# A hybrid decoder layer on one core: fewer products in the mLSTM heads, an unsplit value product and a mask filled by GpSimd in the prompt attention, and moved steps in the later stages

## The chip, the core and the metric

One core of a Trainium2 chip runs the whole program. The time is the device time of one execution, in microseconds; the shown figure is the median of three runs. Its engines are TensorE (PE in the profile, with PEld for its weight loads), VectorE (DVE), ScalarE (ACT), GpSimd (POOL) and SyncE (SP, which here only issues DMAs). Each has its own queue of instructions and works it off in order; semaphores make one wait for another.

## The reference

One layer for 1024 prompt positions of one sequence and for 8 decoding sequences of 4 new positions each (32 columns, kept behind the 1024). What matters here:

```python
def mlstm_chunk(carry, xs):           # 4 heads of 128, chunks of 128 positions
    ...
    s = jnp.einsum('bhtd,bhsd->bhts', q, k) * w_intra
    num = w_inter[..., None] * jnp.einsum('bhtd,bhde->bhte', q, c_st) + jnp.einsum('bhts,bhse->bhte', s, v)
    den = w_inter * jnp.einsum('bhtd,bhd->bht', q, n_st) + jnp.sum(s, axis=-1)
    h = num / jnp.maximum(jnp.abs(den), jnp.exp(-m_t))[..., None]
    ...
    n_new = decay[..., None] * n_st + jnp.einsum('bhs,bhsd->bhd', w_s, k)

def fox_prompt(q, k, v, lf):          # 8 heads of 64, blocks of 128 rows
    ...
    logits = logits + fb.transpose(0, 2, 1)[..., None] - f_keys[:, :, None, :]
    logits = jnp.where(kpos[None, :] <= qpos[:, None], logits, -jnp.inf)
    p = jax.nn.softmax(logits, axis=-1)
    return jnp.einsum('bhts,bshd->bthd', p.astype(v.dtype), v)

def merge_out(x, y_m, m_o, g_mh, y_f, gates, w_pa, w_pb, w_out):
    hm = rmsnorm(y_m.astype(x.dtype), g_mh) * jax.nn.sigmoid(m_o).reshape(bn, t, H_M, DV_M)
    a = hm.reshape(bn, t, W_M) @ w_pa
    b = y_f.reshape(bn, t, W_F) @ w_pb
    return x + (jax.nn.sigmoid(ga) * a + jax.nn.sigmoid(gb) * b) @ w_out

def ffn_and_ple(x, p, g_ffn, w_gu, w_down, g_ple, w_ple_gate, w_ple_proj):
    ...
    gate = jax.nn.sigmoid(rmsnorm(x, g_ple) @ w_ple_gate)
    return x + gate * (p.astype(x.dtype) @ w_ple_proj)
```

`fox_sample` is the same attention for the new positions, with keys, values and forget values of 512 earlier positions read from pages of a cache.

## The kernel before

All of it is float32. Most products are made of three: each operand is split into a high half in the reduced format fp32r and the low rest (names that end in h and l, as `wha` and `wla`), and high x high, low x high and high x low are summed. ACT or GpSimd makes a high half by a copy, VectorE or GpSimd the low half by a subtraction. The 1056 columns go in three pieces of 352; 24 products of 352 columns for one output block are called a unit here. The stages run one after the other, each engine with its own part of each, and the order on every engine is written out by hand.

**Stage 2, mLSTM and gate units (213 to 521 us).** Four heads, one after the other. For a head, VectorE weights queries (`qs`), keys (`kws`, `kw`) and scores (`sw`) and runs the chunk states (`states`, `nstates`). TensorE makes numerators in `pA` (L1917, L1919) and, with a matrix of ones, denominators in `pB` (L1920 for the scores, L1922 for the state), then the same for the 32 new positions in `pS` (L1924 to L1930, by sequence). ACT and VectorE turn the denominators into factors (`dd`, L1532, with its reciprocal) while TensorE works on gate units (L1863), and after `h_done` TensorE makes the new states (L1939, L1941).

**Stage 3, prompt attention (521 to 810 us).** Eight heads (g) of eight blocks of 128 rows (i). `logits3` makes the logits of a block against all keys up to it from split halves (L1966, L1967), and a bf16 product of `identb` and `maskb` adds the mask to the block on the diagonal (L1969). `bias3` on VectorE adds the forget row `nF` and takes the maximum in one instruction (L1559), and from it makes the exponent's bias `nb` (L1563). ACT applies the exponential (L1223), TensorE transposes (`turn_p3`, L1978), ACT copies the high half `pth` (`high3`, L1227), VectorE subtracts the low half `ptl` (`low3`, L1568), and for every second block `values3` multiplies with `vh` and `vl` (L1995). Halves of gate units (`FILL`) lie between the blocks in TensorE's queue. GpSimd makes low halves of queries (`low_q`, L902), keys (`low_k`, L908), values (`low_v`, L912) and of weight chunks (`split_chunk`, L842).

**Stage 4, decode attention (810 to 917 us).** 18 gate units are numbered f; `logits4`, `turn_p4`, `values4` for two groups of four sequences stand among them at fixed numbers. `load_pages` on SP brings in the cache pages (`kvg`).

**Stage 5, merge (917 to 1138 us).** Products with w_pb, then w_pa, then w_out (L2105). VectorE squares the mLSTM rows, normalizes them and makes the low halves `actl`; in the second loop it makes `tmp` and its low half `tl` (`low_t`, L1678) per piece t.

**Stage 6** is the FFN, which the change leaves alone. **Stage 7** (1895 to 2031 us) is the gate of the layer embedding: for each unit (c, t), block c of 8 and piece t of 3, TensorE makes gate and projection. For c = 0 it first sums the squares of the piece (`sums7`, L2199), which ACT (`sqa`) and GpSimd (`sqp`, by pairs, three buffers) prepare. ACT makes the scale (`rms7`), then the sigmoid, and VectorE the result `yq` (L1784), which frees the bank for the second unit after.

Of the kernel before, what the change touches and what calls it, by code (L numbers as in the profile page):

```python
# [22 lines left out]
P = 128  # L23
# [25 lines left out]
def program(nc, a, o):  # L49

    ctx = ExitStack()
    with ctx:
# [37 lines left out]
        identb = take("identb", [P, P], BF16)  # L90
        maskb = take("maskb", [P, P], BF16)
# [77 lines left out]
        sw = take("sw", [P, T])  # L169
        kw = take("kw", [P, NCH, DM])  # L170
# [6 lines left out]
        sqn = take("sqn", [P, 2, T])  # L177
        attn2_end = top[0]
# [5 lines left out]
        top[0] = attn3_base  # L184
        nF = take("nF", [P, 2, SEQ])
# [4 lines left out]
        pth = take("pth", [P, 20 * 256], F32R)  # L190
        ptl = take("ptl", [P, 20 * 256], F32R)
        vh = take("vh", [P, NCH, P], F32R)
        vl = take("vl", [P, NCH, P], F32R)
# [3 lines left out]
        mx = take("mx", [P, NCH])  # L197
        fcol = take("fcol", [P, NCH])
# [211 lines left out]
        v_hi = sem("v_hi")  # L410
        v_lo = sem("v_lo")
# [3 lines left out]
        nb_done = sem("nb_done")  # L415
        p_done = sem("p_done")
        tp_mm = sem("tp_mm")
        pt_hi = sem("pt_hi")
        pt_lo = sem("pt_lo")
# [70 lines left out]
        sum5 = again("sum5")  # L490
        rv_done = again("rv_done")
# [53 lines left out]
        assert IN3 % 6 == 0 and UNITS4 == 18  # L545

# [13 lines left out]
        def _(sp):  # L560
# [119 lines left out]
            def load_v(g):  # L680
                if g:
                    sp.wait_ge(v_lo, g)
                sp.dma_start(v3[:], plane(2)[0:SEQ, g * DH:(g + 1) * DH].rearrange("(i p) d -> p i d", p=P)).then_inc(v3_in, 16)
# [10 lines left out]
            def load_pages(g, first, last):  # L694

                for b in range(first, last):
                    for i in range(PAGES):
                        at_p = (g * GB + b) * PAGES + i
                        page = sp.value_load(ptb[0:1, at_p:at_p + 1], min_val=0, max_val=NPOOL - 1)
                        sp.dma_start(kvg[:, b, i, :], a["cache_kv"][bass.ds(page, 1)].rearrange("a p n -> p (a n)")).then_inc(kvg_in[g], 16)  # L700
# [19 lines left out]
            for g in range(HF):  # L720
# [3 lines left out]
                for i in range(NCH):  # L724
                    if i == 2:
                        if g:
                            store_y(g - 1)
                        if g + 1 < HF:
                            load_v(g + 1)
                    for n in chunks_ended(g, i):  # L730
                        load_chunk3(n + 3)
            for n in range(*FILL_END):
                load_chunk3(n + 3)
            sp.wait_ge(pt_in, 16)
            sp.wait_ge(nb_done, NCH * HF)
            load_pages(0, 0, GB // 2)
            store_y(HF - 1)
            sp.wait_ge(y_st, 16 * HF)
# [9 lines left out]
            load_pages(0, GB // 2, GB)  # L748
# [4 lines left out]
            sp.dma_start(gv[:], a["gains"]).then_inc(gv_in, 16)  # L753
            sp.dma_start(yst5[:, :, 0:SEQ], o["yT"].rearrange("(c p) t -> p c t", p=P)[:, :, 0:SEQ]).then_inc(y5_in, 16)
            sp.wait_ge(o4_mm, 1)
            load_pages(1, 0, GB)
# [71 lines left out]
        def _(pool):  # L828
# [20 lines left out]
            nc.gpsimd.memset(identb[:], 0.0).then_inc(pool_own, 1)  # L849
            nc.gpsimd.memset(maskb[:], 0.0).then_inc(pool_own, 1)  # L850
            nc.gpsimd.memset(maskT[:], 0.0).then_inc(pool_own, 1)
            nc.gpsimd.memset(maskS[:], 0.0).then_inc(pool_own, 1)
            pool.wait_ge(pool_own, 5)
            for m in (ident, identb):
                nc.gpsimd.affine_select(out=m[:], in_=m[:], compare_op=ALU.not_equal, fill=1.0, base=0,
                                        pattern=[[-1, P]], channel_multiplier=1)
            nc.gpsimd.affine_select(out=maskb[:], in_=maskb[:], compare_op=ALU.is_ge, fill=NEG, base=0,
# [6 lines left out]
            pool.wait_ge(pool_own, 6)  # L864
# [14 lines left out]
            for g in range(HM):  # L879
# [3 lines left out]
                pool.wait_ge(pool_own, 6 + g + 1)  # L883
# [11 lines left out]
            nc.gpsimd.memset(vh[:, :, DH:].bitcast(F32), 1.0)  # L895
            nc.gpsimd.memset(vl[:, :, DH:].bitcast(F32), 0.0).then_inc(consts, 1)

            def low_q(g, own, value):

                pool.wait_ge(qk_hi, 2 * g + 1)  # L900
                pool.wait_ge(own, value)
# [1355 lines left out]
```

## Time and profile before

| | us |
|---|---|
| median of 3 runs (lowest to highest) | 2028.18 (2027.02 to 2030.33) |
| profiled execution, device time | 2032.48 |
| span of its trace | 2030.8 |
| TensorE busy | 1935.5 (95% of the span) |
| VectorE, GpSimd, ACT busy | 864.7, 577.0, 519.5 |

The profile shows one execution. Busy time is not bound to be on the path that sets the end: TensorE's queue is nearly full, so the other engines count where TensorE waits for them. In rows with idle time, the bracket holds how long the engine stood before the instruction and who released it. The granted clock is a share of TensorE's full speed.

### The profile page before, as it was taken

The numbers are of one execution on the slowest core, as the hardware profiler recorded it, in microseconds if no ns is written. First come the engines' busy times: TensorE is split into PE (matmuls) and PEld (weight loads), VectorE is DVE, ScalarE is ACT, GpSimd is POOL, SyncE is SP. The second block draws the span as 40 slices with busy tenths as digits, with TensorE's granted clock in tenths as the row PEclk, the third lists the DMA queues.
The fourth block names the chain that finished last, engine by engine and source line by source line (L and its number), as shares of the span: only waits on it lengthen the run. The fifth ranks groups of instructions, "written<-read, shape, count | busy, mean of one in ns | idle before, by whom it ended". The sixth has DMA issues, their size and how long they took to land.

```text
span 2030.8 us, 29755 instructions
## 1 busy us (share of the span) xinstructions
PE 1935.5 (95%) x11759; PEld 1834.2 (90%) x11759; DVE 864.7 (43%) x1426; ACT 519.5 (26%) x848; POOL 577.0 (28%) x374
## 2 busy tenths in 40 slices
PE   5999999999889899988889999999999999999999
PEld 3687999999888888768889999999999999999899
DVE  3350033534467675205753344244434443443643
ACT  4421133332445453116322201000100110011710
POOL 2221112211323232112245622233222332232421
PEclk8999999889999999989999999999999999999999
DMA  5122514433434433664421211111111111111021
GB/s 175 37 74 77 171 43 160 150 103 85 134 82 105 106 95 126 215 251 172 153 87 41 83 52 42 41 41 56 47 41 41 45 58 42 41 63 37 23 91 40
DMA packets 174535, 179.14 MB, mean 88 GB/s; under 512 B 22170, under 2 KB 146142, under 8 KB 174450
## 3 DMA queue, kind: packets, MB, share of 16 engines
q1 hardware_dynamic: 156652, 155.93, 25.3%
q10 hardware_dynamic: 16774, 21.90, 3.0%
q8 instruction: 58, 0.95, 0.2%
q0 software_dynamic: 1024, 0.13, 0.1%
q14 instruction: 27, 0.22, 0.0%
HBM read 143.06 MB, written 34.87 MB: 88 GB/s over the span
## 4 chain that ended last, share of the span: by engine, by line
PE 82%; DVE 7%; issue 4%; ACT 3%; DMA 2%; SPq 1%; ACTq 1%; POOL 0%; DVEq 0%; POOLq 0%
PE pair L2105 29%; PE bank L2105 21%; PE bank L1863 13%; PE bank L1814 5%; PE pair L1995 2%; PE pair L1814 2%; DVE yb L1577 2%; DVE ptl L1568 1%; DMA kvg<-in_cache_kv 1%; PE pair L1793 1%; PE pair L1978 1%; PE pair L1875 1%; DVE actl L1422 1%; PE pair L2045 1%; PE pair L1832 1%
## 5 line engine op out<-in xcount | busy, mean ns | idle before, releaser
L1863 PE MATMUL bank<-acth,fwh 128*128 128x352 f32 x768 | 266.7, 347 | 2.9 <-DVE nrow L1545 1.9
L1863 PE MATMUL bank<-acth,fwl 128*128 128x352 f32 x768 | 255.0, 332 | 0.0
L1863 PE MATMUL bank<-actl,fwh 128*128 128x352 f32 x768 | 254.7, 332 | 0.0
L2105 PE MATMUL bank<-acth,wha 128*128 128x352 f32 x640 | 210.9, 330 | 16.5 <-DVE actl L1639 5.3
L2105 PE MATMUL bank<-acth,wla 128*128 128x352 f32 x640 | 208.4, 326 | 0.0
L2105 PE MATMUL bank<-actl,wha 128*128 128x352 f32 x640 | 208.2, 325 | 0.0
L842 POOL TENSOR_TENSOR fwl<-fraw,fwh 128x1024 fp32r<-128x1024 f32 x32 | 77.3, 2417 | 388.9 <-ACT fwh L1088 388.9
L2105 PE MATMUL pair<-hh,whb 128*128 128x352 f32 x528 | 170.7, 323 | 0.0
L2105 PE MATMUL pair<-hl,whb 128*128 128x352 f32 x528 | 169.2, 320 | 0.0
L2105 PE MATMUL pair<-hh,wlb 128*128 128x352 f32 x528 | 169.0, 320 | 0.0
L1863 PEld LDWEIGHTS bank<-acth,fwh 128*128 128x128 f32 x768 | 151.4, 197 | 9.8 <-issue 5.4
L965 POOL CAST wha<-raw 128x1024 fp32r<-128x1024 f32 x46 | 52.5, 1140 | 377.2 <-PE bank L2105 167.1
L1756 DVE TENSOR_TENSOR XR<-XR,pair 128x352 f32<-128x352 f32 x264 | 131.8, 516 | 63.1 <-PE pair L2105 63.0
L1863 PEld LDWEIGHTS bank<-actl,fwh 128*128 128x128 f32 x768 | 151.7, 198 | 1.7
L1863 PEld LDWEIGHTS bank<-acth,fwl 128*128 128x128 f32 x768 | 150.7, 196 | 0.0
L2105 PEld LDWEIGHTS bank<-acth,wha 128*128 128x128 f32 x640 | 122.5, 191 | 18.7 <-issue 16.2
L1374 ACT CAST hh<-un 128x352 fp32r<-128x352 f32 x66 | 32.2, 488 | 419.0 <-DVE un L1733 388.2
L965 POOL CAST whb<-raw 128x1024 fp32r<-128x1024 f32 x44 | 48.7, 1107 | 308.0 <-PE pair L2105 307.5
L2105 PEld LDWEIGHTS bank<-actl,wha 128*128 128x128 f32 x640 | 122.9, 192 | 0.3
L2105 PEld LDWEIGHTS bank<-acth,wla 128*128 128x128 f32 x640 | 122.5, 191 | 0.0
L967 POOL TENSOR_TENSOR wla<-raw,wha 128x1024 fp32r<-128x1024 f32 x46 | 114.2, 2483 | 3.7
L2105 PE MATMUL pair<-acth,whb 128*128 128x352 f32 x352 | 113.5, 322 | 0.0
(352 smaller groups left out, 4563.4 us busy)
## 6 DMA issues: line engine op xcount, KB each, us to landing
raw<-in_w_gu SPq DMA_DIRECT2D x44, 512.0 KB, 3.9
fraw<-in_w_in SPq DMA_DIRECT2D x32, 512.0 KB, 5.0
kvg<-in_cache_kv SPq DMA_DIRECT2D x32, 512.0 KB, 7.6
scratch_zT<-fout ACTq DMA_DIRECT2D x24, 528.0 KB, 3.5
raw<-in_w_down SPq DMA_DIRECT2D x22, 512.0 KB, 3.7
gs<-scratch_zT SPq DMA_DIRECT2D x16, 528.0 KB, 3.7
wraw<-in_w_in SPq DMA_DIRECT2D x12, 512.0 KB, 5.2
xr<-in_xT SPq DMA_DIRECT2D x6, 704.0 KB, 12.7
```

The source lines that it names most:

```text
L842: nc.gpsimd.tensor_tensor(fwl[j][:], fraw[j][:], fwh[j][:].bitcast(F32), ALU.subtract).then_inc(f_lo, 1)
L965: nc.gpsimd.tensor_copy(hi, raw[j][:]).then_inc(pool_own, 1)
L967: nc.gpsimd.tensor_tensor(lo, raw[j][:], hi.bitcast(F32), ALU.subtract).then_inc(w_split, 1)
L1374: nc.scalar.copy(hh[:, j, t * TW:(t + 1) * TW], un[:, v % 2, :]).then_inc(h_hi, 1)
L1422: nc.vector.tensor_tensor(actl[:, k, cut(t)], xn[:, k % 2, :], acth[:, k, cut(t)].bitcast(F32), ALU.subtract).then_inc(xlo_done, 1)
L1568: nc.vector.tensor_tensor(pt_view(ptl, i), tp_bank(i), pt_view(pth, i).bitcast(F32), ALU.subtract).then_inc(pt_lo, 1)
L1577: own.step(nc.vector.reciprocal(y, pC[DH:, m * 256:(m + 1) * 256]))
L1756: nc.vector.tensor_tensor(x, x, BANK[4 + u % 4][:, 0:TW], ALU.add).then_inc(x6_done, 1)
L1814: ins = nc.tensor.matmul(BANK[u % 3][0:rows, :], x[:, k, i * P:i * P + rows], w[:, q % 2, k, :], start=n == 0, stop=n == 3 * KC - 1)
L1863: ins = nc.tensor.matmul(BANK[u % 2][:, 0:TW], w[j][:, k, :], x[:, k, cut(t)], start=m == 0, stop=m == 3 * KC - 1)
L1995: ins = nc.tensor.matmul(pC[:, m * 256 + skip:(m + 1) * 256], v[:, j, :], x[:, base + j * 256 + skip:base + (j + 1) * 256], start=n == 0, ...
L2105: ins = nc.tensor.matmul(out, w[i](k), x[j](k), start=n == 0, stop=n == total - 1)
```

## The change

The causal mask of the prompt attention is filled into a copy of the forget row by GpSimd and not added by TensorE, and steps of five stages change. Part by part:

- mLSTM: VectorE makes `dn`, the scores plus queries times chunk state, and TensorE sums over it with ones in three products, 128, 384 and 512 columns. `nqs` does the same for the new positions in one product, and the new normalizer is one product with the weights in `rB`.
- Prompt attention: `masked_row` fills the mask into `nFd`, a copy of `nF`. `bias3` handles the block on the diagonal with `nFd`, the others with `nF`, and takes the larger maximum. The mask product is gone. Weights `pt` and values `vf` are no longer split: `values3` is one full float32 product per key tile; `low3` and `low_v` are gone.
- Decode attention: pages are loaded in pieces, the first four in the last but one head. `logits4(0)` stands at unit 4 in place of 6, and what follows it moves likewise. The scan of the forget values and the wait for stores `y_st` change their place.
- Merge: GpSimd squares the mLSTM rows and makes `tl` for t = 2; the sums stand after block 1 in place of 2, ACT's and VectorE's steps follow.
- Last stage: `ORDER7` puts unit (1, 0) ahead of (0, 1).

The core of the diff:

```diff
+        ORDER7 = [(0, 0), (1, 0), (0, 1), (0, 2), (1, 1), (1, 2)] + [(c, t) for c in range(2, KC) for t in range(NT)]
...
+            def masked_row(g):
+                pool.wait_ge(nF_in[g % 2], 16 * (g // 2) + 16)
+                if g >= 2:
+                    pool.wait_ge(nb_done, 8 * (g - 1))
+                nc.gpsimd.affine_select(out=nFd[:, g % 2].rearrange("p (c t) -> p c t", t=P), in_=nF[:, g % 2].rearrange("p (c t) -> p c t", t=P),
+                                        compare_op=ALU.is_ge, fill=NEG, base=0, pattern=[[0, NCH], [-1, P]],
+                                        channel_multiplier=1).then_inc(nFd_done, 1)
...
+                    if i == 2 and g + 1 < HF:
+                        masked_row(g + 1)
...
+                own.step(nc.vector.tensor_tensor(dn[:, P:].rearrange("p (c t) -> p c t", t=P), qs[:, P:SEQ].rearrange("p (c t) -> p c t", t=P),
+                                                 nstates[:, 0:NCH - 1].unsqueeze(2).to_broadcast([P, NCH - 1, P]), ALU.mult))
+                dve.wait_ge(sw_done, g + 1)
+                nc.vector.tensor_tensor(dn[:, P:], dn[:, P:], sw[:, P:SEQ], ALU.add)
...
-                own.step(nc.vector.tensor_tensor_reduce(out=lg[:, i % 2, 0:(i + 1) * P], in0=lg_bank(i), in1=nF[:, g % 2, 0:(i + 1) * P],
-                                               scale=1.0, scalar=-3.0e38, op0=ALU.add, op1=ALU.max,
-                                               accum_out=mx[:, i:i + 1]))
+                n = i * P
+                ins = nc.vector.tensor_tensor_reduce(out=lg[:, i % 2, n:n + P], in0=lg_bank(i)[:, n:n + P], in1=nFd[:, g % 2, n:n + P],
+                                                     scale=1.0, scalar=-3.0e38, op0=ALU.add, op1=ALU.max,
+                                                     accum_out=(mxd if i else mx)[:, i:i + 1])
+                if i:
+                    own.step(nc.vector.tensor_tensor_reduce(out=lg[:, i % 2, 0:n], in0=lg_bank(i)[:, 0:n], in1=nF[:, g % 2, 0:n],
+                                                            scale=1.0, scalar=-3.0e38, op0=ALU.add, op1=ALU.max,
+                                                            accum_out=mx[:, i:i + 1]))
+                    own.step(nc.vector.tensor_tensor(mx[:, i:i + 1], mx[:, i:i + 1], mxd[:, i:i + 1], ALU.max))
...
-            def square_mlstm(h):
-                dve.wait_ge(h5_in, 16)
-                nc.vector.tensor_tensor(rvm[:, h, :], hst5[:, h, :], hst5[:, h, :], ALU.mult).then_inc(hsq, 1)
...
+                if t == 2:
+                    return
...
-                for b in range(DB):
-                    ins = nc.tensor.matmul(pB[:, b:b + 1], kws[:, b, :], ones[0:NS, 0:1], start=True, stop=True)
-                ins.then_inc(us_mm, 1)
+                nc.tensor.matmul(pB[:, 0:DB], k_in[0:NS, NCH, :], rB[0:NS, SEQ + DS - 1::DS], start=True, stop=True).then_inc(us_mm, 1)
...
-                    if last:
-                        ins = nc.tensor.matmul(out[:, n - P:n], identb[:], maskb[:], start=False, stop=True)
...
-                    for v, x in ((vh, pth), (vh, ptl), (vl, pth)):
-                        ins = nc.tensor.matmul(pC[:, m * 256 + skip:(m + 1) * 256], v[:, j, :],
-                                               x[:, base + j * 256 + skip:base + (j + 1) * 256], start=n == 0, stop=n == total - 1)
-                        n += 1
+                    ins = nc.tensor.matmul(pC[:, m * 256 + skip:(m + 1) * 256], vf[:, j, :],
+                                           pt[:, base + j * 256 + skip:base + (j + 1) * 256], start=j == 0, stop=j == 2 * m + 1)
...
-                if f == 6:
+                if f == 4:
```

On TensorE, the end of the denominators of one mLSTM head, before (x8 counts instructions in a row):

```order
L1917 MATMUL pair<-sw,v_in 128x128
L1919 MATMUL pair<-qs,states 128x128
L1920 MATMUL pair<-sw,ones 128x128
L1922 MATMUL pair<-qs,nstates 128x128
L1924 MATMUL pair<-sw,v_in 128x32
L1926 MATMUL pair<-qs,cst 128x4 x8
L1928 MATMUL pair<-sw,ones 128x32
L1930 MATMUL pair<-qs,ncur 128x4 x8
```

and now the same place:

```order
L1948 MATMUL pair<-sw,v_in 128x128
L1950 MATMUL pair<-qs,states 128x128
L1951 MATMUL pair<-sw,ones 128x128
L1952 MATMUL pair<-dn,ones 128x384
L1953 MATMUL pair<-dn,ones 128x512
L1955 MATMUL pair<-sw,v_in 128x32
L1957 MATMUL pair<-qs,cst 128x4 x8
L1959 MATMUL pair<-sw,ones 128x32
L1960 MATMUL pair<-nqs,ones 128x32
```

The products with `ones` and `nstates` that alternated with the numerators are gone, and three wide ones on `dn` stand behind them.

On VectorE, block i = 3 of one head of the prompt attention, before (ISA is the reduction and its read-out):

```order
L1558 MEMSET waits 128x1
L1559 ISA lg,mx<-pair,nF 128x512
L1559 ISA mx 128x1
L1563 SCALAR_TENSOR_TENSOR nb<-mx,fcol 128x1
L1568 TENSOR_TENSOR ptl<-pair,pth 128x3x128
```

and now the same block, with `mxd` for the diagonal:

```order
L1588 MEMSET waits 128x1
L1590 ISA lg,mxd<-pair,nFd 128x128
L1590 ISA mxd 128x1
L1594 ISA lg,mx<-pair,nF 128x384
L1594 ISA mx 128x1
L1597 TENSOR_TENSOR mx<-mx,mxd 128x1
L1601 SCALAR_TENSOR_TENSOR nb<-mx,fcol 128x1
```

The subtraction for `ptl` has left the block; a second reduction with its read-out and the maximum of the two have come in ahead of `nb`.

On ACT, from the last squares of the last stage, before (rv is a scale, gn the sigmoid of a unit, yq its store):

```order
L1384 ACTIVATE acth<-XR,gv 128x352
L1387 ACTIVATE sqa<-XR 128x352
L1391 ACT_TABLE_LOAD
L1391 ACTIVATE rv_196<-pair,epsc 128x352
L1393 ACT_TABLE_LOAD
L1393 ACTIVATE rv_196<-rv_196 128x352
L1400 ACT_TABLE_LOAD
L1400 ACTIVATE gn_187<-gn_187 128x352
L1402 DMA out_outT<-yq 128x352
L1391 ACT_TABLE_LOAD
L1391 ACTIVATE rv_197<-pair,epsc 128x352
L1393 ACT_TABLE_LOAD
```

and now:

```order
L1406 ACTIVATE acth<-XR,gv 128x352
L1409 ACTIVATE sqa<-XR 128x352
L1413 ACT_TABLE_LOAD
L1413 ACTIVATE rv_196<-pair,epsc 128x352
L1415 ACT_TABLE_LOAD
L1415 ACTIVATE rv_196<-rv_196 128x352
L1421 ACT_TABLE_LOAD
L1421 ACTIVATE gn_187<-gn_187 128x352
L1423 DMA out_outT<-yq 128x352
L1421 ACTIVATE gn_191<-gn_191 128x352
L1423 DMA out_outT<-yq 128x352
L1413 ACT_TABLE_LOAD
```

The second scale now stands behind the sigmoid and the store of a second unit of the first piece.

## Rows read from the trace of the kernel before

**Rows 1.** The page's engines: busy us (share of the span) x instructions.

```profile
PE 1935.5 (95%) x11759; PEld 1834.2 (90%) x11759; DVE 864.7 (43%) x1426; ACT 519.5 (26%) x848; POOL 577.0 (28%) x374
```

**Rows 2.** TensorE's waits: line, waited for, us in total, times, longest us.

```profile
PE pair L1995 <- DVE ptl L1568: 14.6, 7, 2.3
PE pair L1966 <- DVE nb L1563: 12.1, 19, 1.8
...
PE pair L2045 <- DMA kvg<-in_cache_kv: 8.3, 2, 7.1
PE bank L2105 <- DVE tl L1678: 7.0, 1, 7.0
...
PE bank L2105 <- DVE actl L1654: 5.1, 1, 5.1
```

**Rows 3.** Timeline of TensorE, one mLSTM head: start us, us, instruction.

```profile
283.29 0.38 PE L1917 MATMUL pair<-sw,v_in 128*128 128x128 f32 x2
...
290.08 0.40 PE L1924 MATMUL pair<-sw,v_in 32*128 32x32 f32 x2
...
292.62 2.54 PE L1930 MATMUL pair<-qs,ncur 128*128 128x4 f32 x16
...
308.53 1.84 PE L1941 MATMUL pair<-ones,kws 32*128 32x1 f32 x16
```

**Rows 4.** Timeline of VectorE, the same head.

```profile
296.34 1.26 DVE L1532 TENSOR_TENSOR dd<-dd,nmB 128x1056 f32<-128x1056 f32 x1 [17.43 <-ACT dd L1192]
297.63 6.75 DVE L1533 RECIPROCAL dd<-dd 128x1056 f32<-128x1056 f32 x1
```

**Rows 5.** Windows: stretch, length, busy us of each engine, granted clock, DMA share, GB/s.

```profile
293.90:300.75 6.85, 6.85 (x27) 6.85 (x27) 4.37 (x2) 1.11 (x2) 0.00 (x0) 0.51 0.00 0
310.90:314.35 3.45, 3.45 (x13) 3.45 (x13) 1.91 (x5) 0.00 (x0) 0.35 (x1) 0.51 0.70 202
```

**Rows 6.** Timeline of TensorE in a head of the prompt attention.

```profile
592.33 0.23 PE L1969 MATMUL pair<-maskb,identb 128*128 128x128 bf16 x1
592.39 1.04 PE L1978 MATMUL pair<-ident,lg 128*128 128x128 f32 x8
...
595.79 0.39 PE L1995 MATMUL pair<-pth,vh 128*128 128x256 f32 x1 [2.05 <-DVE ptl L1568]
...
598.70 0.30 PE L1978 MATMUL pair<-ident,lg 128*128 128x128 f32 x1
```

**Rows 7.** VectorE's groups, 521 to 810 us: count, busy, mean ns, idle before.

```profile
L1563 DVE SCALAR_TENSOR_TENSOR nb<-mx,fcol 128x1 f32<-128x1 f32 x64 | 28.6, 447 | 2.3
...
L1568 DVE TENSOR_TENSOR ptl<-pair,pth 128x1024 fp32r<-128x1024 f32 x8 | 9.8, 1223 | 13.9 <-ACT pth L1227 13.9
```

**Rows 8.** Timelines of VectorE and GpSimd at 645 us.

```profile
645.58 2.21 DVE L1563 SCALAR_TENSOR_TENSOR nb<-mx,fcol 128x1 f32<-128x1 f32 x1
...
645.38 2.39 POOL L902 TENSOR_TENSOR qst<-qd,qst 64x1024 fp32r<-64x1024 f32 x1 [3.68 <-ACT qst L1234]
```

**Rows 9.** GpSimd's groups over the span, a fill of a mask.

```profile
L859 POOL TENSOR_SCALAR_AFFINE_SELECT maskT<-maskT 128x128 f32<-128x128 f32 x1 | 0.3, 288 | 0.0
```

**Rows 10.** TensorE's groups, 827 to 900 us, decode attention.

```profile
L2045 PE MATMUL pair<-kvg,qz 128*32 128x512 f32 x64 | 12.7, 968 | 8.3 <-DMA kvg<-in_cache_kv 8.3
L2063 PE MATMUL pair<-kvg,pT 128*32 128x512 f32 x32 | 3.6, 595 | 0.0
```

**Rows 11.** Timeline of VectorE in the merge.

```profile
1003.20 0.52 DVE L1678 TENSOR_TENSOR tl<-tmp,th 128x352 f32 x1
```

**Rows 12.** Timelines of TensorE, GpSimd and ACT in the last stage.

```profile
1930.27 0.43 PE L2105 MATMUL bank<-acth,wha 128*128 128x352 f32 x1 [1.53 <-DVE yq L1784]
...
1935.14 0.32 PE L2105 MATMUL bank<-acth,wha 128*128 128x352 f32 x1
...
1903.57 2.38 POOL L1035 TENSOR_TENSOR sqp<-sqa 128x352 f32<-128x352 f32 x2 [2.27 <-PE pair L2199]
...
1904.81 0.50 ACT L1387 ACTIVATE sqa<-XR 128x352 f32<-128x352 f32 x1 [0.57 <-POOL sqp L1035]
```

More of the change, by code:

```diff
@@ L177, in program @@
         sqn = take("sqn", [P, 2, T])
+        nqs = take("nqs", [P, NS])
         attn2_end = top[0]
@@ L184, in program @@
         top[0] = attn3_base
+        top[0] += 4 * D * 4
+        nFd = take("nFd", [P, 2, SEQ])
         nF = take("nF", [P, 2, SEQ])
@@ L189, in program @@
         lg = take("lg", [P, 2, SEQ])
[L190 to L193, printed above, removed]
+        pt = take("pt", [P, 20 * 256])
+        vf = take("vf", [P, NCH, P])
         yb_at = top[0]
@@ L197, in program @@
         mx = take("mx", [P, NCH])
+        mxd = take("mxd", [P, NCH])
         fcol = take("fcol", [P, NCH])
@@ L490, in program @@
         sum5 = again("sum5")
+        t_lo2 = again("t_lo2")
         rv_done = again("rv_done")
@@ L694, in load_pages @@
             def load_pages(g, first, last):
[L696 to L700, printed above, removed]
+                for n in range(first, last):
+                    at_p = g * GB * PAGES + n
+                    page = sp.value_load(ptb[0:1, at_p:at_p + 1], min_val=0, max_val=NPOOL - 1)
+                    sp.dma_start(kvg[:, n // PAGES, n % PAGES, :], a["cache_kv"][bass.ds(page, 1)].rearrange("a p n -> p (a n)")).then_inc(kvg_in[g], 16)
             for i in range(2):
@@ L848, in _ @@
             nc.gpsimd.memset(ident[:], 0.0).then_inc(pool_own, 1)
-            nc.gpsimd.memset(identb[:], 0.0).then_inc(pool_own, 1)
-            nc.gpsimd.memset(maskb[:], 0.0).then_inc(pool_own, 1)
             nc.gpsimd.memset(maskT[:], 0.0).then_inc(pool_own, 1)
             nc.gpsimd.memset(maskS[:], 0.0).then_inc(pool_own, 1)
[L853 to L857, printed above, removed]
+            pool.wait_ge(pool_own, 3)
+            nc.gpsimd.affine_select(out=ident[:], in_=ident[:], compare_op=ALU.not_equal, fill=1.0, base=0,
                                     pattern=[[-1, P]], channel_multiplier=1)
@@ L922, in _ @@
             low_k(0)
+            masked_row(0)
             pool.wait_ge(pt_in, 16)
@@ L958, in _ @@
                 split_chunk(n + 2)
-            before = 8 + HM
+            before = 6 + HM
             def split_piece(n, count, j, hi, lo):
@@ L1393, in rms7 @@
                 nc.scalar.activation(rv[t][:], rv[t][:], ACT.Exp, scale=-0.5).then_inc(rv7_done, 1)
-            for v in range(NT * KC):
-                c, t = v // NT, v % NT
+            for v, (c, t) in enumerate(ORDER7):
                 if c == 0:
@@ L1966, in logits3 @@
                     nc.tensor.matmul(out[:, c:c + w], q, khh[:, g % 2, c:c + w], start=True, stop=False)
-                    ins = nc.tensor.matmul(out[:, c:c + w], q, klo[:, g % 2, c:c + w], start=False, stop=not last)
-                    if last:
-                        ins = nc.tensor.matmul(out[:, n - P:n], identb[:], maskb[:], start=False, stop=True)
+                    ins = nc.tensor.matmul(out[:, c:c + w], q, klo[:, g % 2, c:c + w], start=False, stop=True)
                 ins.then_inc(lg_mm, 1)
@@ L1975, in turn_p3 @@
                 if free:
-                    pe.wait_ge(pt_lo, free)
+                    pe.wait_ge(pt_out, free)
                 for j in range(i + 1):
@@ L2201, in _ @@
             pe.wait_ge(pt7_lo, 2)
-            for v in range(NT * KC):
-                c, t = v // NT, v % NT
+            for v, (c, t) in enumerate(ORDER7):
                 if c == 0:
```

154 lines of the change are left out of this document (78 added, 76 removed).

## The prediction

> **What bounds the kernel now.** I read the page's engine table first: TensorE is busy for 1935.5 us [rows 1], so most of the time is work in TensorE's queue, and only what shortens that queue, a wait of TensorE, or a stretch at the lower clock can move the end. Next the list of TensorE's waits [rows 2]: five of them the diff touches, 47.1 us in all. 14.6 are the value products of the prompt attention waiting for `ptl`, 12.1 its logits waiting for `nb`, 8.3 the decode logits waiting for cache pages, 7.0 and 5.1 the merge waiting for the low halves `tl` and `actl`. Last the timeline and the windows of single stages, for the rows below. The profiled execution took 2032.5 us, 1.7 more than its span and 4.3 above the median of the runs, 2028.2. The terms are read from the profiled execution; I take their sum off the median, since the difference between the two is far below the width of the range.
>
> **mLSTM heads (4 heads of equal pattern).** Between 283.29 and 290.08 TensorE runs 30 products of 128 columns, 0.226 us each [rows 3]; 15 of them make the numerator and stay, 15 make the denominator (3.40 us). Those become three products, 1024 columns in all, at the same rate 8 x 0.226 = 1.81: -1.6. The eight four-column products on `ncur` (2.54 us) become one of 32 columns; the nearest row is the 32-column product at 290.08, at most 0.40: -2.2. The eight one-column products at 308.53 (1.84 us) become one, about 0.3 by the same row: -1.5. Together -5.3 a head, **-21** for four. The price is on VectorE: two instructions of 896 columns for `dn`, at most 1.26 each by the row of 1056, and a small one for `nqs`. They go where VectorE lies idle for 17.43 us ahead of `dd` [rows 4], and `dn` is needed only after the numerators, so I cost them at nothing; if that cover were gone they would cost 2.5 a head.
>
> The clock: behind the denominators the granted clock is 0.51 for 6.85 us, the lower of its two levels (1.2 GHz), and again for 3.45 us at 310.9 [rows 5]; ahead of each TensorE has just run the narrow products that go. Without the drops 3.4 and 1.7 us a head would come back. But beside the first drop runs a chain for which TensorE's next step waits: `dd`, the reciprocal, and an ACT and a VectorE instruction about as wide as `dd`, 1.26 + 6.75 + 2 x 1.2 = 10.4 [rows 4]. The filler in TensorE's queue meanwhile is 48 gate products at 0.162 ([rows 12], 4.87 for 30) and two small means, some 8.8. So what the drop now takes beyond 10.4 is all that can be had. I take -1 a head for both drops, **-4**; ends 0 and -10 (the second whole, a quarter of the first). Stage: **-25**.
>
> **Prompt attention (8 heads).** Four things. (a) The mask product goes: 0.06 us from start to start [rows 6], 64 times: -4. (b) The values: the last group of a head is 24 split products in 2.91 us [rows 6]; now it is seven of 256 columns in full precision and one of 128. At the rate of [rows 3] that is 15 x 0.226 = 3.39. A head has 20 key tiles, 16 of them 256 columns wide and 4 of 128, so 36 x 0.226 = 8.1 against 2.91 x 20/8 = 7.3: +0.8 at most. Wider products share their start; I take +0.6 a head, +5. (c) The wait for `ptl` [rows 2]: the subtraction that made it, 1.22 us in the widest block [rows 7], is gone, but ACT's copy of the same block stays and stands last. I leave half of the wait: -7. (d) The bias step is split: in 56 of 64 row blocks there is one more reduction, over 128 columns, its read-out and a `max` of one column, about +0.33 between the logits and `nb`. TensorE is seen to wait for `nb` 19 times [rows 2]; 19 x 0.33 = +6. Stage: **0**.
>
> The unknown is what GpSimd does to (d). `nb`, one column, takes 0.447 us on average [rows 7], and took 2.21 at 645.58, where it began 0.2 after a GpSimd subtraction of 2.39 and ended with it [rows 8]. The change adds a second VectorE instruction of that kind, the `max` of `mx` and `mxd`, to 56 chains, and a GpSimd instruction, the mask fill over 1024 columns. The trace has a fill of 128 columns only, 0.288 [rows 9]: between that and eight times it, 2.3, I take 1.2. The fill stands next to other long GpSimd work, so `max` and `nb` can be held one after the other. In return the low halves of `v`, as wide as half a fill but with two inputs, leave GpSimd, so I leave its load as it was. Ends for the stage: -14 (the whole wait for `ptl` goes, no chain grows) and +26 (all 56 chains exposed, 18.5, and half of the 28.6 that `nb` takes now, 14, held once more, less 7).
>
> The Trainium skill, "SBUF — State Buffer", section "Who interferes with whom", says that a VectorE instruction with two SBUF inputs contends with a GpSimd instruction that reads SBUF, and that the one that issues later is blocked until the other is done. The trace agrees for `nb` (2.21 us). By that rule fill and `max` both count, which speaks against this change, and the sum keeps its 0 for the stage; if the fill held nothing, the stage would stand at about -4.
>
> **Decode attention.** Pages 0 to 13 are loaded earlier, and the first logits start two units earlier. The two waits for pages, 8.3 [rows 2], go if the pages land in time. The 64 logits products take 12.7 us, the 32 value products of the same width 3.6 [rows 10], so 12.7 - 7.2 = 5.5 are too much; a product behind a wait running at the lower clock would do that, and then it goes with the waits. **-14**, ends -5 (the second wait goes in part) and -15.
>
> **Merge.** The squares of the mLSTM rows move to GpSimd and their sums start one column block earlier, so the wait of 5.1 shrinks to about 2: -3, and a stretch of lower clock behind it like the one at 310.9 [rows 5], -1.5. In the loop on the mLSTM side VectorE ends last by 7.0 [rows 2]; one of its nine instructions per column block, 0.52 us [rows 11], moves to GpSimd, eight times, less some overlap: -3.5. **-8**, ends -3 and -13. The moved steps stand in GpSimd's queue ahead of weight splits that TensorE needs, hence the poor end.
>
> **Gate of the last stage.** Unit (1,0) moves ahead of (0,1). A unit takes TensorE 4.87 us (1930.27 to 1935.14). The sums for the second third of the rows now come behind that unit, and GpSimd's next pairs of squares wait for those very sums (idle 2.27, released by TensorE's L2199); ACT's square at 1904.81 waits for such a pair [rows 12]. ACT works in order, so its last squares, and behind them the first scale factor, which unit (0,0) needs before its bank comes free, are about 4.9 later, and TensorE's third unit with them. Two later waits between units shrink, but the third sums now stand behind that delayed unit. **+5.5**, ends -5 (the waits go and nothing is late) and +7.
>
> Constants that GpSimd no longer builds, and renumbered semaphores: nothing, no wait of TensorE hangs on them.
>
> Sum: -25 + 0 - 14 - 8 + 5.5 = -41.5; 2028.2 - 41.5 = 1986.7, **1987**.
>
> **Rivals.**
> 1. *The attention gains in full.* No chain to `nb` grows, since the subtraction leaves VectorE more room than the split takes: stage -14 instead of 0. For it: the wait for `ptl` is the longest of [rows 2]. Against: `max` lengthens a chain that TensorE already waits for. 1987 - 14 = 1973.
> 2. *The waits turn up elsewhere.* The pages land late for the earlier logits (-5 in place of -14), the merge gains 3 only, the clock nothing: 1987 + 9 + 5 + 4 = 2005. For it: the loads come forward only in part, the logits by two whole units.
> 3. *The reordered gate gives what its order would without the held squares*: -5 in place of +5.5, 1976.5. Against: GpSimd's row, released by TensorE's sums.
> 4. *Slower than before.* GpSimd's long instructions hold both `max` and `nb`. Place: between logits and `nb`, in all eight heads. To be slower it has to give back 41.5, 5.2 us a head: more than two full holds of 2.4 in each head that TensorE sees whole. At its bound of +26 it gives 2013; at two such holds and the 0.33 of every block, 8 x 4.8 + 18.5 - 7 = 50, it would be 2037. Against: filler units lie between the blocks, and TensorE waits for `nb` in 19 of 64 now.
> 5. *The change does not do what it says*: the mask fill is the part named, but most of the sum lies in other parts, so that fill and split alone, undone, would be worth only what (a) and (d) are, +2. This moves no time.
>
> **How the numbers follow.** The forecast (1978 to 1996) has 0.50; rivals 1 and 3 together (below 1978) 0.20; rival 2 (1996 to 2012) 0.20; from there to 2024 0.05, mostly the bound of the attention; no change 0.02; rival 4 0.03. The range for 8 in 10 leaves out about a tenth at each end. Its lower end joins rival 1 to the better ends of clock and merge (-14 - 6 - 5): 1962. Its upper end is rival 2 with a little of the attention's loss: 2010. A measurement of this kernel can tell about 0.2%, 4 us, from no change: faster 0.95, same 0.02, slower 0.03.
>
> **What would show it.** Right: denominators in 1.8 us in place of 3.4, and a head of the mLSTM some 6 us shorter; no wait of the value products above 1.2; no wait for pages, and some 3.6 for each group's logits; the third gate unit starting some 4.6 later against the start of the stage. Wrong: a fill of over 2 us, `nb` or `max` with a mean above 0.6, a head of the attention that takes longer than before, or a wait for pages ahead of the first logits.

## The result and the profile after

The changed kernel takes 1994.05 us, median of four runs (1992.70 to 1996.53); the kernel before, on the same chip and also four runs, 2029.26 (2027.02 to 2032.00). The ratio is 0.9827, with a 95% interval of 0.9810 to 0.9844: 35.2 us faster. Forecast were 1987, in a range of 1962 to 2010.

The profiled execution has a span of 1991.9 us. First the page's engine line, which answers to [rows 1]: 31.6 us less of busy TensorE.

```profile
PE 1903.9 (96%) x11327; PEld 1797.8 (90%) x11327; DVE 855.4 (43%) x1530; ACT 520.4 (26%) x848; POOL 595.2 (30%) x381
```

Then TensorE's list of waits, which answers to [rows 2] (line, waited for, us in total, times, longest us):

```profile
PE pair L1992 <- DVE nb L1601: 13.5, 14, 3.0
...
PE bank L2126 <- DVE yq L1815: 10.7, 1, 10.7
...
PE pair L2017 <- ACT pt L1249: 6.0, 7, 0.9
...
PE pair L2066 <- DMA kvg<-in_cache_kv: 5.2, 1, 5.2
PE bank L2126 <- DVE tl L1707: 4.0, 1, 4.0
PE bank L2126 <- DVE actl L1685: 3.9, 1, 3.9
```

The wait of the value products has shrunk from 14.6 to 6.0 and now hangs on ACT's copy. The wait for `nb` has not shrunk: 12.1 in 19 pieces has become 13.5 in 14. A wait for pages is still there, and those for `yq`, before 4.8 in two pieces (one of them in [rows 12]), have become one of 10.7.

The clearest view is where each stage begins. I took the start of TensorE's first product of each stage from the timeline of both kernels; the differences are the time of a stage.

| Stage, from its first product (the projections from the start of the span) to the next stage's | before | after | change | forecast |
|---|---|---|---|---|
| projections | 213.6 | 211.9 | -1.7 | 0 |
| mLSTM heads and gate units | 317.3 | 293.0 | -24.4 | -25 |
| prompt attention | 279.4 | 272.7 | -6.7 | 0 |
| decode attention | 112.3 | 105.8 | -6.5 | -14 |
| merge | 211.7 | 206.7 | -4.9 | -8 |
| FFN | 760.6 | 760.6 | 0.1 | 0 |
| last stage, to its last product | 131.2 | 136.3 | +5.2 | +5.5 |
| sum | 2026.0 | 1987.1 | -38.9 | -41.5 |

The projections have the same products in both, and in all later kernels, where they took between 211.1 and 213.5, so -1.7 is the scatter of that stage. The prompt attention with the changed kernel's own instructions took 271.7 to 274.5 in five traces. The other small differences are to be read against this. The total is near the forecast partly by luck: the attention came out 6.7 better than forecast and the decode attention 7.5 worse. The sum is a little more than that of the medians because the profiled execution of before lies 3 to 4 us above its median.

### The profile page after: what moved, and what is told of

It reads as the page before. It is cut to its first block, busy times and chain, and to the rows that moved or that the text cites. A ratio compares the mean times of both kernels' runs of the same rounds, so it can differ in the third digit from the quotient of the medians.

```text
span 1991.9 us, 29020 instructions
## 1 busy us (share of the span) xinstructions
PE 1903.9 (96%) x11327; PEld 1797.8 (90%) x11327; DVE 855.4 (43%) x1530; ACT 520.4 (26%) x848; POOL 595.2 (30%) x381
## 3 DMA queue, kind: packets, MB, share of 16 engines
q0 software_dynamic: 1024, 0.13, 0.1%
## 4 chain that ended last, share of the span: by engine, by line
PE 81%; DVE 8%; issue 3%; ACT 3%; DMA 2%; POOL 1%; SPq 1%; ACTq 0%; DVEq 0%; POOLq 0%
PE pair L2126 29%; PE bank L2126 22%; PE bank L1894 11%; PE bank L1845 5%; PE pair L2017 3%; PE pair L1845 2%; DVE yb L1613 2%; PE pair L2002 1%; DVE dd L1561 1%; PE pair L1824 1%; DMA nmB<-scratch_rows 1%; DVE lg L1594 1%; DMA kvg<-in_cache_kv 1%; DVE mx L1597 1%; DVE actl L1443 1%
## 5 line engine op out<-in xcount | busy, mean ns | idle before, releaser
L2126 PE MATMUL bank<-acth,wha 128*128 128x352 f32 x640 | 210.3, 329 | 20.0 <-DVE yq L1815 10.7
```

What stands on the lines that cost most here:

```text
L2126: ins = nc.tensor.matmul(out, w[i](k), x[j](k), start=n == 0, stop=n == total - 1)
```

## The experiments

Each run is compared with the kernel before on the same chip, and its trace by the same stage starts. Where a stage is given two numbers, they are this kernel's and the changed kernel's.

**The mask back on TensorE.** The question was what the part named in the change is worth by itself.

```diff
-                    own.step(nc.vector.tensor_tensor(mx[:, i:i + 1], mx[:, i:i + 1], mxd[:, i:i + 1], ALU.max))
+                own.step(nc.vector.tensor_tensor_reduce(out=lg[:, i % 2, 0:(i + 1) * P], in0=lg_bank(i), in1=nF[:, g % 2, 0:(i + 1) * P], ...
...
+                    if last:
+                        ins = nc.tensor.matmul(out[:, n - P:n], identb[:], maskb[:], start=False, stop=True)
```

> The changed kernel (1994 us) with one part undone: the causal mask is again a product on TensorE, nF alone feeds one reduction per row block, and neither the fill on GpSimd nor the max of mx and mxd is there. Theory A, the fill and the max cost more than the mask product did, since GpSimd's long instructions hold max and nb 21 times where they held nb 10 times: TensorE's waits for nb in the prompt attention fall from 13.5 to about 5, the 64 products cost 4.2, the kernel takes about 1990. Rival B, the holds lie beside filler work and the product was the dearer: the waits for nb stay above 10 and the kernel takes about 1998.

Measured: 1985.23, ratio 0.9771 (0.9746 to 0.9797). The prompt attention takes 261.1 in place of 272.7. TensorE's wait for `nb` in this kernel:

```profile
PE pair L1976 <- DVE nb L1585: 4.8, 9, 1.1
```

Theory A holds, and by more than it said: the fill with what it brings along (the second reduction and the `max`) costs 11.6 us more in its stage than the mask product. The rest of the change there (unsplit weights and values) gives 18.3, the way from 279.4 to 261.1. The two errors of the forecast lay on opposite sides.

What holds VectorE is seen in the timelines of VectorE, GpSimd and TensorE in the changed kernel (start, us, instruction), at two places, which answer to [rows 8]:

```profile
608.91 2.27 DVE L1601 SCALAR_TENSOR_TENSOR nb<-mx,fcol 128x1 f32<-128x1 f32 x1
...
608.83 2.34 POOL L849 TENSOR_TENSOR fwl<-fraw,fwh 128x1024 fp32r<-128x1024 f32 x1 [13.12 <-ACT fwh L1110]
611.12 1.09 POOL L920 TENSOR_SCALAR_AFFINE_SELECT nFd<-nF 128x1024 f32<-128x1024 f32 x1
...
611.24 0.50 PE L1992 MATMUL pair<-khh,qst 128*128 128x512 f32 x1 [3.04 <-DVE nb L1601]
```

`nb`, begun 0.08 after GpSimd's weight split, ends with it at 611.18, and TensorE's next logits stood for 3.04 us. The second place is the fill itself:

```profile
640.88 0.16 DVE L1597 TENSOR_TENSOR mx<-mx,mxd 128x1 f32<-128x1 f32 x1
644.27 1.04 DVE L1597 TENSOR_TENSOR mx<-mx,mxd 128x1 f32<-128x1 f32 x1
...
644.21 1.09 POOL L920 TENSOR_SCALAR_AFFINE_SELECT nFd<-nF 128x1024 f32<-128x1024 f32 x1
```

The `max` takes 0.16 when nothing holds it and 1.04 under a fill that began 0.06 earlier. Over the stage, VectorE's groups (count, busy, mean ns):

```profile
L1597 DVE TENSOR_TENSOR mx<-mx,mxd 128x1 f32<-128x1 f32 x56 | 27.4, 490 | 1.9
L1601 DVE SCALAR_TENSOR_TENSOR nb<-mx,fcol 128x1 f32<-128x1 f32 x64 | 23.9, 373 | 2.3
```

Counting in the trace those that took over 0.1 longer than the median of their group, 21 were held (16 `max`, 5 `nb`), for 28.4 us beyond their medians, against 10 and 14.3 before. Each of the 21 ended with a GpSimd instruction: 19 with subtractions of the kinds that were there before, two with a fill, for 1.2 us together. So the fill hardly holds anything itself; with two instructions in each block there is more to be hit. The holds alone don't explain the 11.6 either: with the mask on TensorE, `nb` was still held 15 times for 20.3 us, more than before, and TensorE waited for it only 4.8 us.

**Max and nb with one tensor input.** To tell the hold from the length of the chain: the same arithmetic, with the second operand given as a column scalar. `nb` needs two instructions for it.

```diff
-                    own.step(nc.vector.tensor_tensor(mx[:, i:i + 1], mx[:, i:i + 1], mxd[:, i:i + 1], ALU.max))
+                    own.step(nc.vector.tensor_scalar(mx[:, i:i + 1], mx[:, i:i + 1], mxd[:, i:i + 1], None, ALU.max))
...
-                nc.vector.scalar_tensor_tensor(out=nb[:, i:i + 1], in0=mx[:, i:i + 1], scalar=f, in1=f,
-                                               op0=ALU.add, op1=ALU.subtract, reverse1=True).then_inc(nb_done, 1)
+                own.step(nc.vector.tensor_scalar(mx[:, i:i + 1], mx[:, i:i + 1], f, f, ALU.add, ALU.subtract))
+                nc.vector.tensor_scalar(nb[:, i:i + 1], mx[:, i:i + 1], -1.0, None, ALU.mult).then_inc(nb_done, 1)
```

> The changed kernel with max and nb of the bias step written with one tensor input each: max takes mxd as a column scalar, nb is made of two instructions with the column of F as a scalar, one more than before, so each of the 64 chains is some 0.15 longer where nothing holds it. Theory A, GpSimd holds only instructions with two tensor inputs in SBUF: no instruction of the bias step takes over 0.5 us, TensorE's waits for nb fall from 13.5 to about 8, the kernel takes about 1989. Rival B, every small VectorE instruction on SBUF is held while GpSimd works: about as many are held as now, 21, and the kernel takes about 1997.

Measured: 1989.43, ratio 0.9790 (0.9761 to 0.9820); the stage 269.0 in place of 272.7. The groups of VectorE:

```profile
L1601 DVE TENSOR_SCALAR mx<-mx,fcol 128x1 f32<-128x1 f32 x64 | 17.5, 273 | 2.3
...
L1597 DVE TENSOR_SCALAR mx<-mx,mxd 128x1 f32<-128x1 f32 x56 | 12.0, 214 | 2.0
L1602 DVE TENSOR_SCALAR nb<-mx 128x1 f32<-128x1 f32 x64 | 9.8, 154 | 2.2
```

Of these 184 instructions none took over 0.28: no hold is left, where GpSimd worked as much as before. So the hold is shown to hang on the second operand being given as a tensor. The Trainium skill, "SBUF — State Buffer", section "Who interferes with whom", says that a VectorE instruction with at most one SBUF input, outside the 2-port modes, does not contend with GpSimd, and that one with two does where GpSimd reads SBUF. The traces agree: none of 184 held here, 21 of 120 in the changed kernel. But TensorE's waits for `nb` stayed, against the 8 that theory A expected:

```profile
PE pair L1992 <- DVE nb L1602: 14.6, 14, 1.6
```

The chain is now longer in every block (0.273 + 0.214 + 0.154 in place of 0.16 + 0.22, 0.26 more): as many waits as in the changed kernel, the longest 1.6 in place of 3.0. The 3.7 us lie elsewhere: TensorE's busy time in the stage falls from 249.0 to 244.3, and the two stretches of 3.4 us at a granted clock of 0.50, which the changed kernel has there, are gone. So theory A is right on the holds, and its 1989 came out though the wait that it named did not fall.

**Max and nb in one instruction.** Hence a third form, with the fill and the two reductions kept, but one instruction behind them. It leaves out adding and taking away F; the softmax is the same for any common shift of a row.

```diff
-                    own.step(nc.vector.tensor_tensor(mx[:, i:i + 1], mx[:, i:i + 1], mxd[:, i:i + 1], ALU.max))
+                    nc.vector.tensor_scalar(nb[:, i:i + 1], mx[:, i:i + 1], mxd[:, i:i + 1], -1.0, ALU.max, ALU.mult).then_inc(nb_done, 1)
...
-                nc.vector.scalar_tensor_tensor(out=nb[:, i:i + 1], in0=mx[:, i:i + 1], scalar=f, in1=f,
-                                               op0=ALU.add, op1=ALU.subtract, reverse1=True).then_inc(nb_done, 1)
```

> The changed kernel with the mask still filled by GpSimd, but max and nb in one VectorE instruction with one tensor input (the larger of mx and mxd, negated, without adding and taking away F): nothing in the bias step can be held, and the chain behind the second reduction is 0.2 us in place of 0.4. Theory A, what the fill cost against the mask product (11.6 in the stage) was the holds and the additional max: the prompt attention takes about 261 in place of 272.7, the kernel about 1983. Rival B, it was the second reduction of every row block: the stage stays at 267 or more, the kernel at about 1989.

Measured: 1980.07, ratio 0.9747 (0.9728 to 0.9765); the stage 257.6, even less than theory A said. TensorE's waits in it:

```profile
PE pair L2013 <- ACT pt L1249: 6.0, 7, 0.9
PE pair L1988 <- DVE nb L1597: 4.0, 7, 0.6
```

This kernel has the mask on GpSimd and is 3.5 us shorter in the stage than the one with the mask on TensorE and the old `nb`. The like pair for fill and second reduction is the last kernel below, with the mask on TensorE and the same kind of single instruction: 256.8, so they cost 0.8 net of the mask product, which is within the scatter. Of the 11.6, then, about 10.8 was the additional `max` together with the further holds on it and on `nb`. This does not tell the longer chain from the holds, but the runs show that both count. Neither this kernel nor the one with scalars has holds, and the 0.43 us more that `max` and `nb` take there in most blocks cost 11.4 in the stage; and without the holds that kernel still gained 3.7 on the changed one, though its chain is 0.26 longer.

**The sums of squares ahead of the reordered units.**

```diff
-                if c == 0:
-                    sums7(t)
-                    pe.wait_ge(xp_lo, KC * t + KC)
+                if v < NT:
+                    sums7(v)
+                if c == 0:
+                    pe.wait_ge(xp_lo, KC * t + KC)
```

> The changed kernel with the sums of squares of the last stage taken out of the reordered units: the sums of piece 1 stand again directly behind unit (0,0) and those of piece 2 behind unit (1,0); the order of the units stays. Theory A, the stage lost its 5 us because ACT's squares waited through GpSimd's pairs for sums that stood behind a whole unit: the third unit starts 21.5 us after the start of the stage in place of 26.0, the wait of 10.7 for yq falls to about 4, the stage takes some 128 in place of 136.3, the kernel about 1986. Rival B, the new order of the units itself makes the first scale late: the third unit stays at 26, the kernel within 2 us of 1994.

Measured: 1988.76, ratio 0.9789 (0.9764 to 0.9815); the last stage 127.8 in place of 136.3 (131.2 before). In the changed kernel GpSimd and ACT stood exactly where the forecast put it, which answers to [rows 12], and TensorE's third unit with them:

```profile
1864.22 1.82 POOL L1057 TENSOR_TENSOR sqp<-sqa 128x352 f32<-128x352 f32 x2 [7.04 <-PE pair L2220]
...
1865.19 0.50 ACT L1409 ACTIVATE sqa<-XR 128x352 f32<-128x352 f32 x1 [5.07 <-POOL sqp L1057]
...
1876.76 0.63 PE L2126 MATMUL bank<-acth,wha 128*128 128x352 f32 x1 [10.69 <-DVE yq L1815]
```

GpSimd's pair waits 7.04 for TensorE's sums, ACT's square 5.07 for the pair, and the third unit 10.69 for the result that hangs on all of it. With the sums ahead, the same wait is

```profile
1874.26 0.40 PE L2126 MATMUL bank<-acth,wha 128*128 128x352 f32 x1 [3.37 <-DVE yq L1815]
```

and the new order of units then does gain: 3.4 us against before. The order itself was not the fault, its sums were.

**The load of yst behind the pages.**

```diff
-            sp.wait_ge(y_st, 16 * HF)
-            sp.dma_start(yst5[:, :, 0:SEQ], ...).then_inc(y5_in, 16)
             sp.wait_ge(o4_mm, 1)
             load_pages(1, 0, GB * PAGES)
+            sp.wait_ge(y_st, 16 * HF)
+            sp.dma_start(yst5[:, :, 0:SEQ], ...).then_inc(y5_in, 16)
```

> The changed kernel with one load moved: the 2 MB of attention outputs for the merge (yst) are asked for behind the 16 pages of the second decode group, not ahead of them. Theory A, the pages land late because these 2 MB went ahead of them: the wait of TensorE for pages falls from 5.2 to about 1, the second group's logits take 3.6 in place of 5.5, the kernel takes about 1988. Rival B, the pages need their 30 us whatever goes ahead: the wait stays above 4, the kernel within 2 us of 1994.

Measured: 1988.09, ratio 0.9796 (0.9764 to 0.9827); the decode attention 98.3 in place of 105.8. In the changed kernel SP asked for `yst` (2 MB) 1.2 us ahead of the pages, and the second logits stood 5.24 and then ran at 5.60 us for 32:

```profile
813.19 0.43 SPq L761 DMA_DIRECT2D yst<-scratch_yT  x1
814.39 1.48 SPq L704 DMA_DIRECT2D kvg<-in_cache_kv  x2
...
847.32 5.60 PE L2066 MATMUL pair<-kvg,qz 128*32 128x512 f32 x32 [5.24 <-DMA kvg<-in_cache_kv]
```

Over the first 4 us of these 32 the granted clock is 0.50. Without `yst` ahead, the pages, issued from 816.38 on, are there in time and the granted clock is 1.00:

```profile
843.40 1.12 PE L2062 MATMUL pair<-lf,selF 64*128 64x512 f32 x2
844.45 3.64 PE L2066 MATMUL pair<-kvg,qz 128*32 128x512 f32 x32
```

The stage is then 14.0 shorter than before, the forecast's own term.

**The low half for t = 2 back on VectorE.**

```diff
-                if t == 2:
-                    return
...
-                    low_t2(2 * n - 12)
-                    low_t2(2 * n - 11)
```

> The changed kernel with one part undone: the low half tl for t = 2 is made by VectorE again, not by GpSimd. Theory A, the move shortened VectorE's loop: TensorE's wait for tl goes back from 4.0 to about 7, the loop on the mLSTM side takes 3 more, the kernel about 1997. Rival B, the loop is shorter for other reasons (sums one block earlier): no change within 1 us in that stage.

Measured: 1999.83, ratio 0.9841 (0.9818 to 0.9865). The loop on the mLSTM side takes 56.9 in place of 52.7, and the wait at its end is

```profile
PE bank L2114 <- DVE tl L1698: 7.3, 1, 7.3
```

Theory A: this move was worth 4.2 in its loop, against -3.5 forecast.

**The last low half of the mLSTM rows earlier.**

```diff
                 if c >= 5:
                     low_mlstm(c - 5)
+                if c == KC - 1:
+                    low_mlstm(3)
...
-            low_mlstm(3)
```

> The changed kernel with one VectorE instruction moved: the last low half of the mLSTM rows (actl of head 3) stands ahead of the three products of block 7 and not behind them. Theory A, the wait of 3.9 ahead of the loop on the mLSTM side is nothing but this place in VectorE's queue, where the instruction is also held by GpSimd's weight split (2.92 us in place of 1.25): the wait goes and the lower clock behind it with it, -4 to -5.5, about 1989. Rival B, the wait is set by the chain of normalization itself: it stays above 2.

Measured: 1994.77, ratio 0.9824 (0.9802 to 0.9846), no change in the time. In the changed kernel the instruction stood behind block 7 and was held as well:

```profile
939.74 2.92 DVE L1685 TENSOR_TENSOR actl<-rvm,acth 128x1056 fp32r<-128x1056 f32 x1
...
939.19 2.35 POOL L978 TENSOR_TENSOR wla<-raw,wha 128x1024 fp32r<-128x1024 f32 x1
```

The same instruction took 1.25 for the heads ahead of it. In its new place the wait for `actl` is gone, as theory A said, but another takes its place:

```profile
PE bank L2127 <- POOL wla L978: 3.5, 2, 2.3
```

TensorE now waits for the weight split, which waits for its load. The products of w_pb took 58.2 in place of 59.8. Theory A is wrong in the number: under a wait of 3.9 lay another of 2.3. The wait that stays above 2, as rival B had it, is one for weights and not for the chain of normalization.

**The mLSTM part alone**, put into the kernel before.

> The kernel before with the mLSTM part of the change alone (dn, nqs and the single products). Theory A, the stage's gain is its own: from the first gate unit to the first logits of the prompt attention some 293 us in place of 317, the kernel -24, ratio about 0.988; the rest of the stages as before. Rival B, part of the 24 came from elsewhere (loads, clock): the kernel -18 or less, ratio 0.991 or more.

Measured: 2007.41, ratio 0.9885 (0.9863 to 0.9907), against 0.988 expected, so the part alone gives 23 of the 35 us. In its trace the stage takes 296.7 in place of 317.3, -20.6; the rest lies in the scatter of other stages.

**All of it together:** the mask on TensorE, `nb` by one instruction with one tensor input, the sums ahead, `yst` behind the pages, the last low half earlier.

> The changed kernel with five edits together: the mask again a product on TensorE; nb made by one VectorE instruction with one tensor input (the negated maximum, without adding and taking away F); the sums of squares of the last stage ahead of the reordered units; yst loaded behind the pages; the last low half of the mLSTM rows (actl) made ahead of the products of block 7. Theory A, the four losses lie in different stages and add up: -9 from the mask, -3 from nb no longer held, -8 in the last stage, -7 in the decode attention, -4 in the merge, so about 1964 where the changed kernel takes 1994, faster than both. Rival B, they share cover (what one frees the next wait takes): about 1975 to 1980.

Measured: 1965.41, ratio 0.9679 (0.9660 to 0.9698). Theory A: the losses lie in different stages and add up. The attention takes 256.8, the decode attention 98.3, the last stage 128.8. That the sum agrees so well is partly luck: the attention gained 15.9 where 12 was said, the low half was worth 4 in the sum and nothing in its own run, and the mLSTM stage, which none of the five touches, took 299.4 in place of 293.0. It is 29 us faster than the changed kernel and 65 faster than before.

## Why the prediction was right, point by point

**mLSTM heads: the mechanism right, the size near, in part by luck.** -24.4 against -25 in this execution; with the part alone it was -20.6, and in all nine other kernels that have it the stage took 293.6 to 299.4, -17.9 to -23.7. The product on `sw` and the two on `dn` take 1.82 us where 15 took 3.40 (timeline of TensorE, answering to [rows 3]):

```profile
405.00 0.39 PE L1951 MATMUL pair<-sw,ones 128*128 128x128 f32 x2
405.22 0.81 PE L1952 MATMUL pair<-dn,ones 128*128 128x384 f32 x2
405.87 1.02 PE L1953 MATMUL pair<-dn,ones 128*128 128x512 f32 x2
406.82 0.40 PE L1955 MATMUL pair<-sw,v_in 32*128 32x32 f32 x2
...
422.30 0.28 PE L1968 MATMUL pair<-rB,k_in 32*128 32x8 f32 x2
```

The clock was the loose term, and the length of the stage largely goes with it: 20.5 us of the stage lay at the lower clock where it took 293.6 and 293.8, 34.1 where it took 299.4, 23.9 in the changed kernel, and 44.4 before. So the runs do not confirm the split into -21 and -4. The drops stay, fewer and at places that move (windows; the value behind the five engines is the granted clock):

```profile
349.60:356.40 6.80, 6.80 (x24) 6.74 (x25) 4.47 (x2) 1.11 (x2) 0.00 (x0) 0.50 0.00 0
411.00:414.40 3.40, 3.40 (x13) 3.40 (x13) 3.37 (x2) 0.00 (x0) 0.00 (x0) 0.50 0.00 0
```

From one head's state products to the next, the first takes 61.7 and the other two 58.2 and 58.1, against 64.9 before. Where a drop is short or gone, TensorE arrives early and waits for `hb`, the end of the reciprocal's chain, 1.7 in one head here and in up to three in other kernels; so the chain is the floor that the forecast said it was.

**Prompt attention: the total near by luck, two terms wrong.** Forecast 0, measured -6.7, out of -18.3 and +11.6. The step that failed is "(c) ... I leave half of the wait" with "(d) ... 19 x 0.33 = +6". What both lack is seen in the way from a block's logits to its `nb`. I took it from the traces, as the mean of the 64 blocks in us: from the end of the last logits product to the start of the first reduction, and from there to the end of `nb`.

| Kernel | until the start | from there to `nb` | together (rounded) | stage |
|---|---|---|---|---|
| before | 0.90 | 1.24 | 2.15 | 279.4 |
| changed | 0.47 | 1.70 | 2.16 | 272.7 |
| max and nb with one tensor input | 0.43 | 1.54 | 1.97 | 269.0 |
| mask on TensorE | 0.32 | 1.33 | 1.65 | 261.1 |
| max and nb in one instruction | 0.30 | 1.07 | 1.37 | 257.6 |
| all together | 0.23 | 0.95 | 1.18 | 256.8 |

In (c) the 48 us of `ptl` that leave VectorE were credited with nothing but the wait for `ptl` itself. They also let the bias step start 0.4 to 0.6 earlier: with the mask on TensorE the wait for `nb` falls from 12.1 to 4.8, and the stretches of lower clock in the stage go (four of 3.4 us before, two in the changed kernel, none there). That is the mechanism of rival 1, hidden by the other term.

In the changed kernel the longer step took the earlier start back, which is why its waits for `nb` look untouched. In (d) the step itself was sized about right: without what the holds took, 28.4 and 14.3 over 64 blocks, it is 1.26 against 1.02, 0.24 longer where 0.33 in 56 of 64 blocks is 0.29. The sum left at nothing that the holds double, 0.22 more a block. The doubt was in the text ("the unknown is what GpSimd does to (d)"), with an end of +26, but not in the sum. The fill took 1.09, where 1.2 was taken. (b) was right: the last group of values takes 3.35 (669.15 to 672.50) where 3.39 was worked out, and at the full clock a head's values take 7.9 us in place of 7.4, 0.5 more where 0.6 was taken. Of the signs of being wrong, one shows: some heads take longer than before. From one head's last value products to the next's, two of seven do, the clearer one 35.5 in place of 34.1.

**Decode attention: right until a transfer was overlooked.** The step that failed is the queue of SP: the change moves the wait for `y_st` and the load of `yst` behind it, and I costed neither against the pages. `yst` went from far ahead of the second group's pages (843.5 and 857.7 before) to 1.2 us ahead of them. With that undone the term is -14.0. The stage came close to rival 2's -5, but not by its cause: the earlier logits had their pages, and it was the second group that waited.

**Merge: mechanism right, size short.** -4.9 against -8. The move of `low_t` gave 4.2 (forecast 3.5). The steps that failed are "shrinks to about 2: -3" and the "-1.5" behind it: the wait for `actl` fell by 1.2, and the lower clock behind it stayed. The instruction waited for in the end stood behind three others in VectorE's queue and was held by GpSimd; and taking that away uncovers a wait for weights.

**Last stage: right.** +5.2 against +5.5, by the very chain: GpSimd's pair, ACT's square, the scale, the third unit at 26.0 after the start of the stage in place of 21.5, 4.5 later where 4.6 was forecast. Rival 3 is out as the change is written; with the sums moved the stage gains 3.4 of its 5. Rival 4's mechanism is there, at 11.6 us and not at the 41.5 that it needed. Rival 5 is right that most of the sum lies in other parts, but its +2 for fill and split measured +11.6.

## What to carry to other kernels

A small instruction in a chain for which TensorE waits is priced by what it adds to every turn of the chain and by what can hold it, not by its width: count the instructions with two SBUF tensor inputs that a change puts in reach of GpSimd, and see whether the second operand can be a column scalar. When a subtraction leaves a busy engine, credit its whole queue, not only the wait that bore its name: see when the next step starts. When steps are reordered, list each transfer and each sum that moves along with them, and ask who stands behind it in its queue.

## What the runs showed of the hardware

A fill (affine select) over 128 x 1024 float32 took 1.09 us and held a VectorE instruction with two tensor inputs to its own end, as GpSimd's subtractions did, though it reads one tensor only; two cases show it (1.04 and 0.51 in place of 0.16). A VectorE instruction of one column with a column scalar as its second operand was never held, in 120 cases, nor was one with a constant, in 64. In the merge, wide VectorE subtractions took longer beside GpSimd's squares:

```profile
880.54 9.27 DVE L1672 TENSOR_TENSOR actl<-yst,acth 128x1408 fp32r<-128x1408 f32 x3 [8.57 <-ACT acth L1332]
...
881.72 11.81 POOL L997 TENSOR_TENSOR rvm<-hst 128x1056 f32<-128x1056 f32 x4
```

The same three subtractions of VectorE took 5.8 us before, without the squares on GpSimd. What sets the place of the stretches at the lower clock in the mLSTM heads stays open: kernels with the same stage up to there had them at different places, and heads between 57.7 and 61.7 us.
